# Compressor's first matrix: which operand is stationary, and in how many column tiles of the array

## The chip, the cores and the metric

The kernel runs on one core of one Trainium2 chip. The metric is the device time of one execution in microseconds (us), and lower is better. TensorE appears in the profile twice, as PE (its matmuls) and PEld (its weight loads). VectorE is DVE, ScalarE is ACT, and SyncE is SP, which here issues nearly all of the loads from HBM.

## The reference, cut to what matters

The program computes two blocks of two layers each, on 256 tokens of width 1024. Only the first block holds the part that is changed, and it holds it once per layer. In both of its layers a "compressor" turns overlapping blocks of 32 tokens into one key and one value per block:

```
def compress(kv, pe, w1, w2):
    B, G, T, dh = kv.shape                       # G = 2, T = 256, dh = 64
    NC = (T - CMP_BLOCK) // CMP_STRIDE + 1       # 15 blocks, length 32, stride 16
    idx = jnp.arange(NC)[:, None] * CMP_STRIDE + jnp.arange(CMP_BLOCK)[None, :]
    blocks = kv[:, :, idx, :] + pe
    flat = blocks.reshape(B, G, NC, CMP_BLOCK * dh)
    return jax.nn.silu(flat @ w1) @ w2           # w1: 2048 x 128, w2: 128 x 64
```

It is called once for the keys and once for the values, each with its own matrices. The two results feed the compressed attention. Beside it each layer has a gated recurrence (HGRN2, in 16 "level" steps below), selected and window attention, three gates (`hgo`, `hz`, `nz`) that are projections of the same input, and an output projection.

## The kernel before, in words

**Tiles and panels.** Activations lie transposed, with features on the 128 partitions and the 256 tokens along the free dimension. Weights come from HBM in panels of 1 MB through three raw slots (`SLOTS`). SP loads them in one fixed order (`LOADS`, load loop with `load_panel`, L2049). A panel can be loaded only when the one three places before it has left its slot (`slot_empty`, L2040). SP issues in order, so a load that waits for its slot holds up all later ones. Most panels are split after landing: ACT casts the high part (`high_part`, L1062) and DVE subtracts the low part (`low_part`, L1531). The split panels are used in three matmuls per product (L419 to L421). The two panels of the compressor's first matrix, `cmp0` (keys) and `cmp1` (values), are used unsplit, as plain float32. They give their raw slots back when the compressor's matmuls have ended (`release`, L381). In the load order `cmp0` and `cmp1` are followed by `hgo0`, `hgo1`, `hz0`, `hz1`, so the load of `hgo1` waits for `cmp0`'s slot, and `hz0` waits for `cmp1`'s.

**Who sets the order.** PE's program is written out by hand. Where PE has finished a piece that another engine must pick up, it appends an entry to an agenda with `todo` (L576). ACT and DVE each walk the agenda in the same order (L1201 and L1669). After an entry each of them also splits the panels whose slots are free at that place (`split_high`, L1073, and `split_low`, L1539). A split whose panel has not landed blocks the engine, and with it all later entries of the agenda.

**The stage around the change.** PE's order in a layer is: projections of queries and keys, with level steps (`level`, L601) strewn between them by `some` (L637); sums of squares; then the compressor's first matrix (`hid`, L699 to L711); one level step (the 14th); the query rotation `qr` (L716 and L717, waiting for DVE's products); one level step (the 15th); the key rotation `kr` (L724 and L725); a half panel of `hgo0` (`gate_chunk`, L619); the last level step; the other half of `hgo0`; the matmuls across the two chunks (`cross`, L734); and the compressor's second matrix (L742 and after, waiting for `hidden_ready`, L740). A level step on PE needs the step two before it to be finished by DVE (`level`, L1637). The first half of `hgo0` is written to PSUM bank 1, so it waits for ACT's copy of `qr0` out of that bank.

**The compressor's first matrix.** The token blocks lie in `M2`, part of the tile that the trace calls probs_t: for each of keys and values, 16 pieces of 128 rows by 32 columns (two groups by 16 block places). For each piece the 128x128 weight piece is stationary and the 32 columns move. Sixteen such matmuls add up in 32 columns of PSUM bank 3, with the hidden features on the partitions. After it the agenda entry `hidden` makes ACT take an exponential of the 64 columns (L1233) and DVE form the SiLU and a copy of it for the values (L1712 to L1722).

A float32 matmul appears in the trace as two weight loads and two matmuls, so 32 matmuls give 64 records in each layer.

Of the kernel before, what the change touches and what calls it, by code (L numbers as in the profile page):

```python
# [8 lines left out]
P = 128  # L9
# [33 lines left out]
def const_table():  # L43

    p = np.arange(P)
    parts = [("ident", np.eye(P)), ("ones", np.ones((P, P))),
             ("head_ones", (p[:, None] // 64 == p[None, :] // 64).astype(float))]

    rot = np.zeros((P, P))
    for h in (0, 64):  # L50
        for d in range(8):
            rot[h + 8 + d, h + d] = -1.0
            rot[h + d, h + 8 + d] = 1.0
    parts.append(("rot", rot))
    inv = (np.float32(500000.0) ** (-np.arange(0, 16, 2, dtype=np.float32) / np.float32(16))).astype(np.float32)
    ang = np.arange(T, dtype=np.float32)[None, :] * inv[:, None]
    cos, sin = np.ones((P, T)), np.zeros((P, T))
    for h in (0, 8, 64, 72):
        cos[h:h + 8] = np.cos(ang.astype(np.float32))
        sin[h:h + 8] = np.sin(ang.astype(np.float32))  # L60
    parts += [("cos", cos), ("sin", sin)]
    t = p[:, None, None] + P * np.arange(NT)[None, :, None]
    seen = (16 * np.arange(16)[None, None, :] + 31 <= t).astype(float)
    parts += [("cmp_neg", ((1 - seen) * NEG).reshape(P, NT * 16)), ("cmp_seen", seen.reshape(P, NT * 16))]
    parts.append(("head16", (p[:, None] // 16 == np.arange(8)[None, :]).astype(float)))
    parts.append(("upper", (p[:, None] <= p[None, :]).astype(float)))
    parts.append(("causal_neg", np.where(p[None, :] > p[:, None], NEG, 0.0)))
    at = 0
    for name, a in parts:
        CONST_COLS[name] = (at, a.shape[1])  # L70
        at += a.shape[1]
    levels = [(p[:, None] == p[None, :])]
    for n in range(1, NLVL):
        h = 1 << (n - 1)
        levels.append((p[:, None] // (2 * h) == p[None, :] // (2 * h)) & (p[:, None] % (2 * h) < h)
                      & (p[None, :] % (2 * h) >= h))
    masks = np.stack(levels, axis=1).astype(np.int32).reshape(P, NLVL * P)
    return np.concatenate([a for _, a in parts], axis=1).astype(np.float32), masks
# [69 lines left out]
def build(nc, a, out):  # L148
# [4 lines left out]
    with ExitStack() as ctx:  # L153
        def sb(name, cols, dt=F32):
            return ctx.enter_context(nc.sbuf_tensor(name, [P, cols], dt))
# [66 lines left out]
        NM = sb("neg_max", 8)  # L222
        SM = sb("prob_sums", 8)
        PP = FK
        ZR = sb("zeros", P)
        NT16 = sb("head_stats", 16)

# [57 lines left out]
        def bank(name):  # L285
            return ps[fills[name][0]]
# [74 lines left out]
        def _(pe):  # L361
# [219 lines left out]
            for l in range(DEPTH):  # L581
# [115 lines left out]
                some(1)  # L697

                pe.wait_ge(blocks_ready, l + 1)  # L699
                begin(f"hid_{l}", 3)  # L700
                for kv in range(2):
                    landed((f"cmp{kv}", l))
                    w1 = raw_panel((f"cmp{kv}", l), 16, P)
                    for jj in range(16):
                        ins = pe.matmul(ps[3][:, kv * 32:(kv + 1) * 32], w1[:, jj, :], M2[:, kv, jj, :, :],  # L705
                                        start=(jj == 0), stop=(jj == 15))
                done(f"hid_{l}", ins)
                release(("cmp0", l))
                release(("cmp1", l))
                todo(("hidden",))  # L710
                some(1)  # L711

                pe.wait_ge(rope_ready, l + 1)
                for j in range(2):
# [4 lines left out]
                                                 start=False, stop=True))  # L719
                    todo(("copy", f"qr{j}"))  # L720
                some(1)
                pe.wait_ge(k_rope_ready, l + 1)
                begin(f"kr_{l}", 4)
                pe.matmul(ps[4][:, :], ident, UK[:, 0:512], start=True, stop=False)  # L724
# [320 lines left out]
        def _(act):  # L1045
# [128 lines left out]
            for l in range(DEPTH):  # L1174
# [26 lines left out]
                for place, step, *arg in agenda[l]:  # L1201
# [6 lines left out]
                    elif step == "blocks":  # L1208

                        name = f"kcvc_{l}"  # L1210
                        full(act, name)
                        src = v3(bank(name), 2)
                        for g in range(2):
                            s = src[64 * g:64 * g + 64]
                            nc.scalar.copy(K2[0:64, :, g, :], s)
                            ins = nc.scalar.copy(K2[64:128, :, g, 0:T - 1], s[:, :, 1:T])
                        ins.then_inc(free(name), 1)
                    elif step == "k_square":
                        name = f"ks_{l}"
                        copy_out(name, KN[:, :], bank(name)[:, :])  # L1220
                        drained(act, name)
                        f(UK[:, 0:512], KN[:, :], ACT.Square).then_inc(ksq_ready, 1)
                    elif step == "gates":
                        name = f"vw_{l}"
                        full(act, name)
                        src = bank(name)[:, 0:304].rearrange("p (n w) -> p n w", n=NT)
                        nc.scalar.copy(vt[:, 1, :, :], src[:, :, 0:P])
                        f(gates, src[:, :, P:152], ACT.Exp, scale=-1.0).then_inc(free(name), 1)
                    elif step == "q_norm":
                        head_rinv([f"qss{j}_{l}" for j in range(2)], HZ[:, :], 64, 1024).then_inc(q_rinv_ready, 1)  # L1230
                    elif step == "k_norm":
                        head_rinv([f"kss_{l}"], UK[:, 512:1024], 64, 512).then_inc(k_rinv_ready, 1)
                    elif step == "hidden":  # L1233
                        full(act, f"hid_{l}")
                        f(SS[:, 0:64], bank(f"hid_{l}")[:, 0:64], ACT.Exp, scale=-1.0).then_inc(hid_exp_ready, 1)
                    elif step == "k_pad":

                        name = f"kr_{l}"
                        full(act, name)
                        src = v3(bank(name), 2)  # L1240
                        for g in range(2):
                            s = src[64 * g:64 * g + 64]
                            nc.scalar.copy(kz[0:64, :, 0, g, :], s)
                            ins = nc.scalar.copy(kz[64:128, :, 1, g, :], s)
                        ins.then_inc(free(name), 1)
                    elif step == "cross":
                        copy_out(f"cross_{l}", AC[:, :], bank(f"cross_{l}")[:, :])
                    elif step == "cmp_kv":
                        name = f"kc_{l}"
                        copy_out(name, KC[:, 0:32], bank(name)[:, 0:32])  # L1250
                        drained(act, name)
                        f(KC[:, 32:64], KC[:, 0:32], ACT.Square).then_inc(kcsq_ready, 1)
                    elif step == "o_square":
                        for g in range(2):
                            copy_out(f"o{g}_{l}", QP[:, g * 512:(g + 1) * 512], bank(f"o{g}_{l}")[:, :])
                        drained(act, f"o1_{l}")
                        f(SQ[:, 0:1024], QP[:, :], ACT.Square).then_inc(osq_ready, 1)
                    elif step == "kc_norm":
                        head_rinv([f"kcss_{l}"], SS[:, 64:96], 64, 32).then_inc(kc_rinv_ready, 1)
                    elif step == "o_norm":  # L1260
                        act.wait_ge(rope_ready, l + 1)
                        head_rinv([f"oss{g}_{l}" for g in range(2)], UK[:, :], P, 1024).then_inc(o_rinv_ready, 1)
                    elif step == "cmp_softmax":
                        act.wait_ge(cmp_shift_ready, l + 1)
                        f(SC[:, :], SC[:, :], ACT.Exp).then_inc(cmp_exp_ready, 1)
                    elif step == "scores":
                        exps(f"n{l}", arg[0], 8 * l + arg[0])
                    elif step == "turned":
                        turned_copies(f"n{l}", arg[0], 8 * l + arg[0])
                    elif step == "sigmoids":  # L1270
                        drained(act, f"hz1_{l}")
                        for dst, src in ((FG, HZ), (SG, SG)):
                            f(dst[:, :], src[:, :], ACT.Sigmoid).then_inc(sig_ready, 1)
                    elif step == "on":
                        mixed_high(l, None, (0, 1))
                        drained(act, f"nz1_{l}")
                        f(VH[:, :], NZ[:, :], ACT.Sigmoid).then_inc(sig_ready, 1)
                        mixed_high(l, [f"on{g}_{l}" for g in range(2)], (2, 3))
# [878 lines left out]
```

## Time and profile before

| what | value |
|---|---|
| runs | 1193.64, 1197.81, 1198.2 us; median 1197.81 us |
| the profiled execution | span 1197.1 us from its first to its last instruction; its time is not given apart from the span |
| busy share of the span | PE 93%, PEld 87%, DVE 59%, ACT 48% |
| mean granted TensorE clock | 0.953 of full speed |
| DMA | 163.88 MB, 137 GB/s on average |
| instructions | 19879 |

A busy share is an average over stages with different limits, and a matmul's modelled end lies after the start of the next one. So the time of a string of matmuls is read here from start to start. The granted clock is 1.00 at 2.4 GHz and 0.50 at 1.2 GHz.

### The profile page before, as it was taken

What the parts mean: (1) busy time and instruction counts of PE and PEld (TensorE: products, weight loads), DVE (VectorE), ACT (ScalarE), POOL (GpSimd) and SP (SyncE); (2) the same over time, 40 slices, a digit from 0 to 9 for tenths busy, and PEclk for the clock granted to TensorE, in tenths of its full rate; (3) what the DMA queues carried; (4) which work ended last, traced back from release to release, by engine and by line L of the source; (5) the groups of instructions that cost most, each with busy time, mean ns of one, the idle gap of its engine ahead of it and who ended that gap; (6) DMA issues with size and microseconds to landing.
All of it is one profiled execution on the core that took longest, in us unless ns stands there. A gap on an engine that the chain in (4) does not pass through costs nothing.

```text
span 1197.1 us, 19879 instructions
## 1 busy us (share of the span) xinstructions
PE 1108.9 (93%) x8321; PEld 1037.9 (87%) x8321; DVE 704.2 (59%) x1009; ACT 579.7 (48%) x816; POOL 4.9 (0%) x13
## 2 busy tenths in 40 slices
PE   4999898798999889798989999999799999999997
PEld 4999676698999677798988999999786699999996
DVE  5556445647566445548685766666543646766674
ACT  4542435546432445545753644544542636455453
POOL 1000000000000000000000000000000000000000
PEclk8999899899998899899999999999996999999998
DMA  8541613135531612134554555556243323655530
GB/s 278 176 113 36 211 36 106 36 106 177 183 107 36 211 62 80 53 121 150 179 176 141 177 176 184 193 184 194 76 146 119 127 91 122 211 176 183 193 115 36
DMA packets 144740, 163.88 MB, mean 137 GB/s; under 512 B 6072, under 2 KB 135424, under 8 KB 144672
## 3 DMA queue, kind: packets, MB, share of 16 engines
q1 hardware_dynamic: 143752, 161.46, 42.0%
q8 instruction: 52, 0.85, 0.3%
q10 hardware_dynamic: 632, 1.29, 0.3%
q0 software_dynamic: 288, 0.14, 0.0%
q14 instruction: 16, 0.13, 0.0%
HBM read 161.84 MB, written 1.05 MB: 136 GB/s over the span
## 4 chain that ended last, share of the span: by engine, by line
PE 74%; DVE 11%; ACT 9%; DMA 2%; issue 2%; SPq 1%; ACTq 0%; DVEq 0%
PE ps L419 21%; PE ps L421 21%; PE ps L420 21%; DVE panels_low L1534 3%; ACT panels_high L1069 3%; PE ps L612 2%; PE ps L499 2%; ACT probs L1055 2%; PE ps L705 2%; PE ps L435 1%; DMA panels<-in_w_in 1%; DVE neg_max L1555 1%; DVE probs L1570 1%; PE ps L523 1%; PE ps L505 1%
## 5 line engine op out<-in xcount | busy, mean ns | idle before, releaser
L419 PE MATMUL ps<-input_high,panels_low 128*128 128x256 f32 x1792 | 523.6, 292 | 33.4 <-DVE input_low L1514 14.2
L420 PE MATMUL ps<-input_low,panels_high 128*128 128x256 f32 x1792 | 515.4, 288 | 0.0
L421 PE MATMUL ps<-input_high,panels_high 128*128 128x256 f32 x1792 | 515.4, 288 | 0.0
L1534 DVE TENSOR_TENSOR panels_low<-panels,panels_high 128x2048 fp32r<-128x2048 f32 (+1 forms) x146 | 330.3, 2265 | 287.5 <-ACT panels_high L1069 279.8
L419 PEld LDWEIGHTS ps<-input_high,panels_low 128*128 128x128 f32 x1792 | 352.1, 196 | 44.5 <-issue 31.2
L420 PEld LDWEIGHTS ps<-input_low,panels_high 128*128 128x128 f32 x1792 | 352.3, 197 | 0.8 <-issue 0.5
L421 PEld LDWEIGHTS ps<-input_high,panels_high 128*128 128x128 f32 x1792 | 351.9, 196 | 0.0
L1069 ACT CAST panels_high<-panels 128x2048 fp32r<-128x2048 f32 (+1 forms) x146 | 274.7, 1883 | 152.3 <-PE ps L421 133.2
L419 PE MATMUL ps<-ffn_hidden_high,panels_low 128*128 128x256 f32 x352 | 100.3, 285 | 4.0 <-DVE ffn_hidden_low L2014 4.0
L420 PE MATMUL ps<-ffn_hidden_low,panels_high 128*128 128x256 f32 x352 | 99.7, 283 | 0.0
L421 PE MATMUL ps<-ffn_hidden_high,panels_high 128*128 128x256 f32 x352 | 99.7, 283 | 0.0
L419 PEld LDWEIGHTS ps<-ffn_hidden_high,panels_low 128*128 128x128 f32 x352 | 67.3, 191 | 4.4 <-issue 4.3
L420 PEld LDWEIGHTS ps<-ffn_hidden_low,panels_high 128*128 128x128 f32 x352 | 67.3, 191 | 0.1
L421 PEld LDWEIGHTS ps<-ffn_hidden_high,panels_high 128*128 128x128 f32 x352 | 67.2, 191 | 0.0
L1055 ACT ACTIVATE probs<-ps,neg_max 128x128 f32<-128x128 f32 (+1 forms) x80 | 32.5, 419 | 71.2 <-DVE neg_max L1555 71.2
L1055 ACT ACTIVATE squares<-residual 128x512 f32<-128x512 f32 x36 | 22.2, 629 | 79.5 <-DVE residual L1580 74.9
L419 PE MATMUL ps<-panels_high,input_low 128*128 128x256 f32 (+2 forms) x192 | 55.5, 289 | 0.0
L420 PE MATMUL ps<-panels_low,input_high 128*128 128x256 f32 (+2 forms) x192 | 55.1, 287 | 0.0
L421 PE MATMUL ps<-panels_high,input_high 128*128 128x256 f32 (+2 forms) x192 | 54.9, 286 | 0.0
L1518 DVE SCALAR_TENSOR_TENSOR squares<-residual,vectors,rinv 128x256 f32<-128x256 f32 x72 | 33.4, 481 | 25.8 <-ACT rinv L1055 25.8
L2000 DVE SCALAR_TENSOR_TENSOR gate_o<-ps,vectors,gate_o 128x255 f32<-128x255 f32 (+1 forms) x96 | 39.6, 475 | 9.6 <-ACT gate_o L1055 8.3
L523 PE MATMUL ps<-k_padded,q_rope 128*128 128x256 f32 (+1 forms) x80 | 35.3, 536 | 9.3 <-ACT probs L1055 7.0
(267 smaller groups left out, 1174.7 us busy)
## 6 DMA issues: line engine op xcount, KB each, us to landing
panels<-in_ffn_up SPq DMA_DIRECT2D x44, 1024.0 KB, 5.1
panels<-in_w_in SPq DMA_DIRECT2D x32, 1024.0 KB, 5.7
panels<-in_ffn_down SPq DMA_DIRECT2D x22, 1024.0 KB, 4.8
panels<-in_mix_w_in SPq DMA_DIRECT2D x20, 1024.0 KB, 5.3
panels<-in_w_out SPq DMA_DIRECT2D x8, 1024.0 KB, 5.3
panels<-in_w_pg SPq DMA_DIRECT2D x8, 1024.0 KB, 6.1
panels<-in_mix_w_out SPq DMA_DIRECT2D x8, 1024.0 KB, 5.8
panels<-in_w_pp SPq DMA_DIRECT2D x2, 1024.0 KB, 4.9
```

What stands on the lines that cost most here:

```text
L419: pe.matmul(dst, w[1], x[0], start=start, stop=False if not kw else True, **kw)
L420: pe.matmul(dst, w[0], x[1], start=False, stop=False if not kw else True, **kw)
L421: return pe.matmul(dst, w[0], x[0], start=False, stop=stop, **kw)
L499: ins = pe.matmul(ps[b][:, 0:T], ones, sq3[:, c, :], start=(c == 0), stop=(c == ND - 1))
L523: pe.matmul(o, q[:, n * P:(n + 1) * P], keys[:, :, 0:w], start=True, stop=True)
L612: ins = pe.matmul(ps[b][:, j * P:(j + 1) * P], KQ[:, s:s + P], QP[:, s:s + P], start=True, stop=True)
L705: ins = pe.matmul(ps[3][:, kv * 32:(kv + 1) * 32], w1[:, jj, :], M2[:, kv, jj, :, :], start=(jj == 0), stop=(jj == 15))
L1055: return nc.scalar.activation(dst, src, func, **kw)
L1069: nc.scalar.copy(high_slots[slot][:, 0:size], raw[n % SLOTS][:, 0:size]).then_inc(high_ready, 1)
L1518: V.scalar_tensor_tensor(xf3[:, c, :], h3[:, c, :], vec(gain, g0 + c), RINV[:, :], ALU.mult, ALU.mult).then_inc(xf_ready, 1)
L1534: V.tensor_tensor(low_slots[slot][:, 0:size], raw[n % SLOTS][:, 0:size], high_slots[slot][:, 0:size].bitcast(F32), ALU.subtract).then_inc( ...
L2000: ins = V.scalar_tensor_tensor(d, ps[2 * par + half][:, j * T:(j + 1) * T - back], VC[:, bass.ds(m + (w0 + (2 - back) * 2 * NFF), 1)], d, ...
```

## The change

The token blocks become the stationary operand and the weights move. A stationary piece has 32 columns and fills one of four column tiles of the array, at columns 0, 32, 64 and 96 (`tile_position`). Piece `jj` goes to tile `jj % 4`, so that each tile adds up four of the sixteen pieces, for keys and then for values. The results are four parts, on four groups of 32 partitions and in 128 columns per kind. ACT copies the 128x256 result to SBUF (agenda entry `hidden_parts`, into 256 columns of a tile that is written only later in the layer). After the query rotation and the 15th level step, two more matmuls per layer, with the copy as stationary operand and a 0/1 matrix of 32 columns moving, add the four parts and turn the result, so that it has the same form as before. The panels are released after the first set of matmuls. The entry `hidden` moves behind the two new matmuls. The table of constants grows by 32 columns.

```
+    parts.append(("sum_of_four", (p[:, None] % 32 == np.arange(32)[None, :]).astype(float)))
...
+        HP = NZ[:, 0:256]
...
-                begin(f"hid_{l}", 3)
+                begin(f"hid4_{l}", 3)
                 for kv in range(2):
                     landed((f"cmp{kv}", l))
                     w1 = raw_panel((f"cmp{kv}", l), 16, P)
                     for jj in range(16):
-                        ins = pe.matmul(ps[3][:, kv * 32:(kv + 1) * 32], w1[:, jj, :], M2[:, kv, jj, :, :],
-                                        start=(jj == 0), stop=(jj == 15))
-                done(f"hid_{l}", ins)
+                        c = 32 * (jj % 4)
+                        ins = pe.matmul(ps[3][c:c + 32, kv * P:(kv + 1) * P], M2[:, kv, jj, :, :], w1[:, jj, :],
+                                        start=(jj < 4), stop=(jj >= 12), tile_position=(0, c), skip_group_check=True)
+                done(f"hid4_{l}", ins)
                 release(("cmp0", l))
                 release(("cmp1", l))
-                todo(("hidden",))
+                todo(("hidden_parts",))
                 some(1)
...
+                drained(pe, f"hid4_{l}")
+                begin(f"hid_{l}", 3)
+                for kv in range(2):
+                    ins = pe.matmul(ps[3][:, kv * 32:(kv + 1) * 32], HP[:, kv * P:(kv + 1) * P],
+                                    const("sum_of_four"), start=True, stop=True)
+                done(f"hid_{l}", ins)
+                todo(("hidden",))
                 pe.wait_ge(k_rope_ready, l + 1)
...
+                    elif step == "hidden_parts":
+                        copy_out(f"hid4_{l}", HP, bank(f"hid4_{l}")[:, 0:256])
```

## Rows read from the trace of the kernel before

**Rows 1.** The page: the chain that ended last, by line.

```profile
PE ps L419 21%; PE ps L421 21%; PE ps L420 21%; DVE panels_low L1534 3%; ACT panels_high L1069 3%; PE ps L612 2%; PE ps L499 2%; ACT probs L1055 2%; PE ps L705 2%; PE ps L435 1%; DMA panels<-in_w_in 1%; DVE neg_max L1555 1%; DVE probs L1570 1%; PE ps L523 1%; PE ps L505 1%
```

**Rows 2.** The chain of waits in both layers' stages: start us, us, what.

```profile
109.96 0.86 PE ps L505 x2
110.82 0.89 PE ps L612 x8
...
121.41 0.38 SPq L2062
121.83 7.75 DMA panels<-in_w_in
129.61 1.91 ACT panels_high L1069
...
378.08 9.80 PE ps L705 x64
```

**Rows 3.** PE's timeline in the first layer: start us, us, instructions, idle before.

```profile
111.55 9.83 PE L705 MATMUL ps<-probs_t,panels 128*128 128x32 f32 x64
121.19 2.06 PE L612 MATMUL ps<-query,forget_key 128*128 128x128 f32 x8
...
129.72 1.02 PE L725 MATMUL ps<-k_rope_terms,consts 128*128 128x512 f32 x2
132.04 0.39 PE L419 MATMUL ps<-input_high,panels_low 128*128 128x256 f32 x1 [1.30 <-ACT q_rope L1060]
...
139.12 1.05 PE L734 MATMUL ps<-query,forget_key 128*128 128x128 f32 x8
...
142.29 0.46 PE L754 MATMUL ps<-decay_diag,values_hg 128*128 128x128 f32 x2 [1.72 <-issue]
```

**Rows 4.** Windows: busy time of PE, PEld, DVE, ACT, POOL; granted clock, DMA, GB/s.

```profile
111.50:115.80 4.30, 4.30 (x41) 4.30 (x41) 4.26 (x7) 0.68 (x2) 0.00 (x0) 1.00 0.00 0
115.80:121.20 5.40, 5.40 (x28) 5.40 (x27) 3.60 (x9) 0.00 (x0) 0.00 (x0) 0.50 0.00 0
121.20:126.00 4.80, 4.80 (x13) 3.19 (x14) 1.20 (x4) 0.22 (x1) 0.00 (x0) 0.50 0.76 236
126.00:131.00 5.00, 4.74 (x17) 2.23 (x15) 2.29 (x1) 3.29 (x2) 0.00 (x0) 1.00 1.10 348
...
140.00:150.00 10.00, 6.49 (x42) 6.27 (x41) 3.38 (x4) 5.13 (x9) 0.00 (x0) 0.83 0.31 105
```

**Rows 5.** ACT's and DVE's timelines in the first layer's stage.

```profile
131.41 1.07 ACT L1060 COPY q_rope<-ps 128x512 f32<-128x512 f32 x2
...
115.54 0.42 DVE L1663 TENSOR_TENSOR forget_key<-forget_key,gate_o 128x256 f32<-128x256 f32 x1
...
121.67 0.20 DVE L1715 TENSOR_SCALAR small<-small 128x64 f32<-128x64 f32 x1 [2.24 <-ACT small L1055]
...
122.75 0.23 DVE L1720 COPY cmp_hidden_rep<-cmp_hidden 128x128 f32<-128x128 f32 x1
...
137.41 0.42 DVE L1663 TENSOR_TENSOR forget_key<-forget_key,gate_o 128x256 f32<-128x256 f32 x1
```

**Rows 6.** Two 64-column tiles: PEld's timeline, one window, and PE's timeline.

```profile
949.93 1.73 PEld L907 LDWEIGHTS ps<-decay_diag,q_nope 128*64 128x64 f32 x32 [0.17 <-issue]
...
949.90:951.60 1.70, 1.70 (x31) 1.67 (x32) 0.76 (x1) 1.68 (x4) 0.00 (x0) 1.00 0.00 0
...
951.73 0.65 PE L551 MATMUL ps<-probs_t,values_hg 128*64 128x256 f32 x4
952.17 0.43 PE L553 MATMUL ps<-probs_t,values_hg 128*64 128x128 f32 x4
```

**Rows 7.** Single operations: a narrow moving operand, a copy out of PSUM, the constants' load.

```profile
L774 PE MATMUL ps<-cmp_k_padded,q_nope 128*128 128x32 f32 x32 | 3.7, 271 | 0.0
...
107.35 0.37 ACT L1227 COPY values_nsa<-ps 128x256 f32<-128x256 f32 x1 [4.96 <-PE ps L421]
...
consts<-in_const_table ACTq DMA_DIRECT2D x1, 676.0 KB, 6.0
```

## The prediction

> **What bounds the kernel now.** I read the page first. The span is 1197.1 us, as the table above has it, and the chain that ended last is mostly PE's three-matmul products; the compressor's line L705 has 2% of it [rows 1]. A line on the chain can be worth its whole time only if nothing else is waiting behind it, so I went on to the chain in order of time around L705, once per layer.
>
> There the reader sees a stage of its own. PE runs the 64 records of L705 from 111.55 to about 121.4 us in the first layer, and for 9.8 us in the second [rows 2, 3]. At 121.41 SP at last issues the loads that waited for the slots of `cmp0` and `cmp1`; 7.75 us of DMA and a cast of 1.91 us follow on the chain [rows 2]. DMA is idle while L705 runs, 0.00 busy, and saturated right after it [rows 4]. ACT sits behind those landings in its agenda, copies `qr0` at 131.41 [rows 5], and only then does PE get bank 1 and start `hgo0` at 132.04, after an idle 1.30 us [rows 3]. So the end of L705 starts a fixed sequence: 121.4 (its end) to 132.04 is 10.6 us, nearly all of it transfers and casts. What ends L705 earlier moves all of it.
>
> The windows give the price of L705 itself: 4.3 us at the full clock with 41 records started, then 5.4 us at half the clock [rows 4]. Its records are about 0.11 us apart at full clock although only 32 columns move: another narrow one, L774, takes 3.7/32 = 0.116 us [rows 7]. A 128x128 weight load per record sets that pace. The clock fell to 1.2 GHz in the middle of it, and came back only at 126.0 during the query rotation [rows 4].
>
> **The change part by part.**
>
> *The matmuls.* There are still 64 records per layer, now with 32 stationary and 128 moving columns. No record before has four tiles at once, so I bound it by neighbours. Alone, a 128-column record takes 0.111 us at full clock (0.89 for 8 [rows 2]): 64 x 0.111 = 7.1 us. Two 64-column tiles are in the trace: 31 records of L907, of the same 128 moving columns, start within 1.70 us, 0.055 apart, so each tile takes one per 0.11 us and the two run together [rows 6]. With four tiles that would be 64/4 x 0.111 = 1.8 us; with two at a time 3.5 us. I take four, because L907 shows a tile to keep its own pace whatever its neighbour does. L551 and L553 say the same: in program order they alternate by tile (two records of L551, two of L553, then the same for the other tile), but all four records of L551 start ahead of all four of L553 [rows 6]. So the tiles don't queue behind each other in program order. I add 0.2 us for entering the tiled arrangement: L907's first weight load has 0.17 us idle before it [rows 6]. So `hid4` takes 2.0 us and ends at 111.55 + 2.0 = 113.6. The Trainium skill, "TensorEngine Tiling (Array Packing)", section "Key Properties", says that a change of tiling mode drains TensorE; that 0.17 us agrees in kind, and is its whole price here.
>
> *The loads.* They are issued at 113.6 in place of 121.4. If nothing else is late, `hgo0` starts 10.6 us later, at 124.2, which is 7.8 us earlier than before.
>
> *What is late next.* PE itself, by a little. The 14th level step needs DVE's 12th, which ends at 115.54 + 0.42 = 115.96 [rows 5]. So PE idles about 2.4 us after `hid4`. From there its work up to `hgo0` is at full clock 2 x 0.89 (level steps) + 6 x 0.86 (rotations; the row has two 512-column records) = 6.9 us [rows 2]; before, the same ran from 121.19 to 130.74, 9.55 us, half of it at 1.2 GHz [rows 3, 4]. The two new matmuls add 4 records x 0.116 = 0.5 us [rows 7]. At full clock PE is through at 115.96 + 7.4 = 123.4, ahead of the 124.2. With as much slow clock as before it is through at 115.96 + 9.55 + 0.5 = 126.0. Which? The 10 us around the idle 1.72 us at 140.6 had a mean of 0.83, that is 3.4 us at 1.2 GHz [rows 3, 4]. 2.4 us of idle should do the same: 3.4 us at half clock cost 1.7 us of dense work. So PE is through at 125.1 and `hgo0` starts 132.04 - 125.1 = 6.9 us earlier (ends: 6.0 and 7.8).
>
> *The copy* of 128x256 costs about 0.37 us [rows 7]. It lies beside the 2.4 us in which PE waits for DVE, and ACT has nothing then: its agenda puts it ahead of the casts that block on the landings. The new wait of PE for it, after the 15th level step, finds it long done. If it were behind the casts, PE would stop there until 123 or later.
>
> *The moved `hidden`.* ACT's exponential now comes after the two copies of `qr`, and ahead of the copies for the padded keys, which are needed much later. DVE's four operations ran in slack, from 121.67 to 122.98, 1.3 us [rows 5]. They move behind the blocking low parts and between its last two level steps. DVE's last level step ended at 137.83 [rows 5], PE's `hgo0` at 139.12 [rows 3]: the slack of 1.29 us covers it just so. I cost it at 0, at most 0.2 us. The second matrix waits for `hidden_ready` only after `cross`, so it meets no new wait.
>
> *The table of constants* grows from 676 KB, 6.0 us to landing, by 16 KB, or 2.4% [rows 7]. That is at most 0.15 us, in the shadow of other first loads; 0.
>
> *Second layer.* The stage repeats, with 9.80 us of L705 on the chain [rows 2]; I take the same gain.
>
> **Sum.** 2 x 6.9 = 13.8, with the small costs 13.8 to 14: I say 13.8. From the profiled execution's own span, 1197.1, that gives 1183.3. What lies around the span is untouched and not shown apart. The runs' median is 0.7 us above that span, so I forecast 1184.0 us.
>
> **The rivals.**
>
> *Two at a time.* The Trainium skill, "TensorE: Matmul & The Clock Gate", section "The mechanism" under Part 3, says that matmuls start and end in program order. By that rule the second record of a tile would hold back the first of the next one. As a mechanism here: only neighbouring records of different tiles overlap, 64 x 0.055 = 3.5 us with the entry 3.7, `hid4` ends at 115.3, and the clock has no idle stretch to fall in. `hgo0` starts at 115.3 + 10.6 = 125.9, 6.1 us earlier: 12.2 in all, 1185.6 us. L551 ahead of L553 [rows 6] speaks against the order, but only for two tiles. 24%.
>
> *One at a time* (the tiling does not do what it says with four tiles): 7.1 us at full clock, `hid4` ends at 118.9, `hgo0` at 129.5, 2.5 us earlier, 5 in all: 1192.8 us. L907 speaks against it. 12%.
>
> *Slower.* The tiles don't overlap, and the narrow stationary operands count as little work, so that the clock is low in the whole stretch: 64 records x 0.222 = 14.2 us, which is 4.4 us per layer longer than 9.8, 8.8 in all: 1206.6 us. It decides from 9.83/64 = 0.154 us per record on. For it: the clock did fall in L705, with 128-column weights but little moving [rows 4]. Against it: in L907's 1.70 us the clock was 1.00 [rows 6], and the first 4.3 us here start at full clock. 4%.
>
> **How the numbers follow.** Four at a time has 58%: 1184.0 us, between 1182 (no slow clock) and 1186 (as much as before). Two at a time 24%, one at a time 12%, slower 4%; 2% remain for a wait that I don't see and that takes the gain. The range takes the first two cases and the spread of the runs (1193.6 to 1198.2, so up to 4 us below the median): 1180 to 1190; one at a time and slower lie outside. 0.5% is 6.0 us, about what a measurement of this kernel can tell from no change. The first two cases and a piece of the third are faster by more: 84%. Most of the third and the unseen wait are within it: 12%. Slower: 4%.
>
> **What would show it.** In the changed kernel: L705's successor with 64 records in about 2 us, four starting close together; SP's issue of the gate panels right after it; PE idle some 2.4 us ahead of the 14th level step; an ACT copy of 0.4 us next to that; `hgo0` starting 10.6 to 11.6 us after the end of `hid4`; DVE's `hidden` operations after its 15th level step. The span from the start of the compressor to `cross`, 27.6 us before [rows 3], should be near 20.7. I am wrong if the 64 records take over 4 us, if the new wait for ACT's copy holds PE, or if `hgo0` starts much later than 11.6 us after `hid4`.

## The result and the profile after

The changed kernel takes 1177.34 us (median of four runs, 1176.19 to 1178.79) against 1196.09 us for the kernel before in the same comparison (1193.64 to 1198.2). The ratio is 0.9849, with a 95% interval of 0.9829 to 0.9870. That is faster, as forecast, but 6.7 us below the forecast of 1184.0 us and outside the range of 1180 to 1190. The profiled execution of the changed kernel has a span of 1174.8 us and a time of 1176.69 us.

First the matmuls. PE's timeline of the changed kernel, in the first layer and in the second (start us, us, instructions, idle before), with the lines that answer to [rows 3]:

```profile
111.46 1.95 PE L708 MATMUL ps<-panels,probs_t 128*32 128x128 f32 x64
115.83 1.16 PE L614 MATMUL ps<-query,forget_key 128*128 128x128 f32 x8 [2.42 <-DVE forget_key L1675]
...
122.46 1.02 PE L735 MATMUL ps<-k_rope_terms,consts 128*128 128x512 f32 x2
124.22 0.39 PE L421 MATMUL ps<-input_high,panels_low 128*128 128x256 f32 x1 [0.73 <-ACT q_rope L1070]
...
131.29 1.06 PE L744 MATMUL ps<-query,forget_key 128*128 128x128 f32 x8
...
134.46 0.46 PE L764 MATMUL ps<-decay_diag,values_hg 128*128 128x128 f32 x2 [1.71 <-issue]
...
369.49 1.74 PE L708 MATMUL ps<-panels,probs_t 128*32 128x128 f32 x56
373.86 1.96 PE L614 MATMUL ps<-query,forget_key 128*128 128x128 f32 x8 [2.42 <-DVE forget_key L1675]
...
382.15 1.02 PE L735 MATMUL ps<-k_rope_terms,consts 128*128 128x512 f32 x2
382.61 0.68 PE L421 MATMUL ps<-input_high,panels_low 128*128 128x256 f32 x1
...
389.65 1.06 PE L744 MATMUL ps<-query,forget_key 128*128 128x128 f32 x8
```

(The view of the second layer ends at 371 us, so its L708 shows the first 56 of the 64 records.) The 64 records take 1.95 us in place of 9.83. PE then idles 2.42 us for DVE's level step, in both layers. `hgo0` starts at 124.22 instead of 132.04, and `cross` at 131.29 instead of 139.12.

The chain of waits behind L708 (start us, us, what) answers to [rows 2]:

```profile
111.53 1.93 PE ps L708 x64
...
113.48 0.38 SPq L2074
...
113.90 7.86 DMA panels<-in_w_in
...
121.78 1.91 ACT panels_high L1079
```

The sequence is the same as before with nearly the same durations (7.86 us of transfers against 7.75), and it begins 7.9 us earlier. From the end of L708 (111.46 + 1.95 = 113.41) to `hgo0` it takes 10.8 us; before it took 10.6.

ACT's and DVE's timelines (answering to [rows 5]) show the new copy in PE's idle time, and the moved `hidden` operations ahead of DVE's last level step:

```profile
113.48 0.37 ACT L1070 COPY nsa_z<-ps 128x256 f32<-128x256 f32 x1 [1.45 <-PE ps L708]
...
115.36 0.42 DVE L1675 TENSOR_TENSOR forget_key<-forget_key,gate_o 128x256 f32<-128x256 f32 x1
...
128.57 0.18 DVE L1727 TENSOR_SCALAR small<-small 128x64 f32<-128x64 f32 x1
...
129.63 0.23 DVE L1732 COPY cmp_hidden_rep<-cmp_hidden 128x128 f32<-128x128 f32 x1
...
130.72 0.42 DVE L1675 TENSOR_TENSOR forget_key<-forget_key,gate_o 128x256 f32<-128x256 f32 x1
```

The windows (columns as in [rows 4]) show the granted clock: the idle and the work up to `hgo0` in the first layer, then the idle, the work right behind it and the rest in the second.

```profile
111.40:113.40 2.00, 2.00 (x66) 1.69 (x64) 1.97 (x3) 0.63 (x1) 0.00 (x0) 1.00 0.00 0
113.40:115.80 2.40, 0.02 (x3) 0.00 (x0) 2.40 (x6) 0.37 (x1) 0.00 (x0) 1.00 0.43 101
115.80:124.20 8.40, 7.65 (x32) 4.43 (x32) 6.21 (x10) 4.32 (x4) 0.00 (x0) 1.00 1.08 348
...
371.40:373.80 2.40, 0.04 (x4) 0.00 (x0) 2.40 (x6) 0.37 (x1) 0.00 (x0) 1.00 0.42 92
373.80:377.40 3.60, 3.54 (x11) 2.51 (x12) 3.45 (x9) 0.53 (x1) 0.00 (x0) 0.53 1.09 369
377.40:383.00 5.60, 5.60 (x24) 3.22 (x22) 3.48 (x2) 4.37 (x5) 0.00 (x0) 1.00 1.04 304
```

In the first layer the clock stayed at 2.4 GHz after the idle. In the second it fell to 1.2 GHz for 3.4 of the 3.6 us after the same idle (a mean of 0.53). There `hgo0` starts 13.1 us after the first record of L708, in the first layer 12.8. This fall is not the rule: three more traces of the same kernel (e2, e11, e15) have the same idle of 2.41 to 2.42 us in both layers, and the clock stays at 1.00 behind it. Here is the window behind it in e2's second layer:

```profile
372.60:378.00 5.40, 5.39 (x26) 3.48 (x26) 3.99 (x9) 1.90 (x1) 0.00 (x0) 1.00 1.09 361
```

One measure is used for all experiments, the **stage**: the time from the first record of the compressor's first matrix to the first of `cross`, in layer 1 and layer 2, read from PE's timeline of each kernel.

| kernel | 64 records, layer 1 | stage, layer 1 | stage, layer 2 |
|---|---|---|---|
| before | 9.83 | 27.57 | 27.82 |
| before, again (e1, e12, e14) | 9.63 to 10.82 | 27.50 to 28.54 | 27.40 to 27.90 |
| after | 1.95 | 19.82 | 20.16 |
| after, again (e2, e11, e15) | 1.95 to 1.96 | 19.72 to 19.90 | 19.75 to 19.90 |
| e3 one tile | 7.17 | 27.33 | 26.22 |
| e4 two tiles | 3.69 | 22.58 | 22.77 |
| e6 tile by tile | 4.33 | 22.12 | 23.20 |
| e5 late loads | 1.96 | 30.21 | 31.81 |
| e7 late split | 1.95 | 18.50 | 20.16 |
| e8 filled idle | 1.95 | 16.01 | 16.01 |
| e9 spread split | 1.95 | 16.40 | 16.40 |

The two stages gave 7.75 + 7.66 = 15.4 us; the forecast was 13.8. But the two traced spans lie 22.3 us apart (1197.1 and 1174.8). The other 6.9 us lie where nothing was changed; e12 to e15 deal with them.

### The profile page after: what moved, and what is told of

Same layout as the page of the kernel before. It is cut to its first block, busy times and chain, and to the rows that moved or that the text cites. A ratio compares the mean times of both kernels' runs of the same rounds, so it can differ in the third digit from the quotient of the medians.

```text
span 1174.8 us, 19899 instructions
## 1 busy us (share of the span) xinstructions
PE 1083.4 (92%) x8329; PEld 1016.0 (86%) x8329; DVE 704.1 (60%) x1009; ACT 580.8 (49%) x818; POOL 5.0 (0%) x13
## 4 chain that ended last, share of the span: by engine, by line
PE 75%; DVE 12%; ACT 9%; issue 2%; DMA 1%; SPq 1%; DVEq 0%; ACTq 0%
PE ps L421 22%; PE ps L422 21%; PE ps L423 21%; DVE panels_low L1546 3%; ACT panels_high L1079 3%; PE ps L614 2%; PE ps L501 2%; ACT probs L1065 2%; PE ps L437 1%; DVE neg_max L1567 1%; DVE probs L1582 1%; PE ps L507 1%; PE ps L525 1%; DMA panels<-in_w_in 1%; PE ps L972 1%
```

## The experiments

**How many tiles run at once: e3, e4.** The rivals differed in this alone. Both experiments keep the operands of the change and use fewer tiles; the copy and the adding matmul shrink to the rows that are used.

```
-                        c = 32 * (jj % 4)
+                        c = 32 * (jj % 1)        # e4: jj % 2
...
-                                        start=(jj < 4), stop=(jj >= 12), tile_position=(0, c), skip_group_check=True)
+                                        start=(jj < 1), stop=(jj >= 15), tile_position=(0, c), skip_group_check=True)
```

> All sixteen pieces go to one 32-column tile, one after another. Theory (concurrency of tiles makes the gain, a tile takes a record per 0.111 us): the 64 records take 7.1 us, 5.2 us more than with four tiles, and the loads start that much later: 2 x 5.2 = 10.4 us slower than the change, near 1188. Rival (narrow stationary operands let the clock fall): the records take up to 14 us, over 20 us slower than the change. Rival (narrow operands alone make the gain, not the tiles side by side): within 2 us of the change.

> The pieces alternate between two 32-column tiles. Theory: 64 records at 0.055 us, 3.6 us, 1.7 us more than with four tiles; the loads decide, so 2 x 1.7 = 3.4 us slower than the change, near 1181. Rival (PE's wait for VectorE after the compressor hides it): within 1 us of the change, since PE idles 2.4 us there.

Measured: e3 1189.13 us, ratio 0.9961 (0.9944 to 0.9977); e4 1180.44 us, ratio 0.9882 (0.9855 to 0.9908). Against the changed kernel beside them (e2, 1176.79 us) that is 12.3 us more where 10.4 was expected, and 3.7 us more where 3.4 was. PE's timeline and two windows of e3:

```profile
111.78 7.17 PE L708 MATMUL ps<-panels,probs_t 128*32 128x128 f32 x64
...
129.71 0.58 PE L421 MATMUL ps<-input_high,panels_low 128*128 128x256 f32 x1 [2.86 <-ACT q_rope L1070]
```

```profile
111.80:119.00 7.20, 7.20 (x66) 7.00 (x66) 7.13 (x14) 0.56 (x2) 0.00 (x0) 1.00 0.00 0
129.70:136.00 6.30, 6.29 (x30) 6.29 (x31) 5.55 (x12) 2.77 (x6) 0.00 (x0) 0.52 1.03 323
```

PE's timeline of e4:

```profile
112.28 3.69 PE L708 MATMUL ps<-panels,probs_t 128*32 128x128 f32 x64
...
126.63 0.39 PE L421 MATMUL ps<-input_high,panels_low 128*128 128x256 f32 x1 [2.02 <-ACT q_rope L1070]
```

One tile, two tiles and four take 7.17, 3.69 and 1.95 us: each tile takes a record per 0.11 us, and four tiles are 7.17/1.95 = 3.7 times as fast as one. The slower rival's premise falls as well: with a stationary operand of 32 columns the clock is 1.00 for all of e3's 7.2 us. Before, with 128 stationary and 32 moving columns, it fell after 4.3 us [rows 4].

e3's stage is the lesson that a shorter matmul is not yet a shorter stage. Its 64 records are 2.7 us shorter in layer 1, and `hgo0` indeed starts 2.6 us earlier after them (129.71 - 111.78 = 17.9 against 20.5). But PE has now waited 2.86 us for ACT's copy, and the clock behind it is 0.52, so that the stage as a whole is only 0.2 us shorter. In layer 2 it is 1.6 us shorter.

**Whether the order of issue matters: e6.** The same four tiles and the same 64 records, but four pieces in a row for one tile.

```
-                        c = 32 * (jj % 4)
+                        c = 32 * (jj // 4)
...
-                                        start=(jj < 4), stop=(jj >= 12), tile_position=(0, c), skip_group_check=True)
+                                        start=(jj % 4 == 0), stop=(jj % 4 == 3), tile_position=(0, c), skip_group_check=True)
```

> As the change, but piece jj goes to tile jj // 4, so that four matmuls in a row (eight records) sit on one tile before the next tile's come. Theory (tiles don't queue in program order, and PE looks far ahead): still about 2 us for the 64 records, time as the change. Rival (matmuls start in program order): tiles overlap only where one ends and the next begins, 64 records in 6 us or more, about 8 us slower than the change, near 1185.

Measured: 1183.07 us, ratio 0.9917 (0.9891 to 0.9943). PE's timeline of e6, the whole group and then only what starts up to 112.37:

```profile
111.92 4.33 PE L708 MATMUL ps<-panels,probs_t 128*32 128x128 f32 x64
...
111.92 0.62 PE L708 MATMUL ps<-panels,probs_t 128*32 128x128 f32 x4
```

PE's timeline of the changed kernel, only what starts up to 111.56:

```profile
111.46 0.32 PE L708 MATMUL ps<-panels,probs_t 128*32 128x128 f32 x4
```

In the changed kernel four records have started within 0.1 us. In e6 it takes 0.45 us for four, at the pace of a single tile. Eight records of one tile take 1.06 us from start to end (the eight of L744 above), so the eight runs of eight records follow each other at (4.33 - 1.06)/7 = 0.47 us, where a run alone holds its tile for 8 x 0.11 = 0.9 us. So neither expectation of 2 us nor of 6 us is met: the tiles do overlap, but a tile is reached only when the one ahead is about half through. A record of the second tile thus starts ahead of the first tile's last three, but not ahead of all of them. The interleaved order of the change is worth 4.33 - 1.95 = 2.4 us per layer.

**Where the gain comes from: e5.** The four tiles stay, but the slots of `cmp0` and `cmp1` are given back only after the two adding matmuls. ACT and DVE keep the place of their splits.

```
-                release(("cmp0", l))
-                release(("cmp1", l))
                 todo(("hidden_parts",))
...
                 done(f"hid_{l}", ins)
+                b, k = fills[f"hid_{l}"]
+                for kv in range(2):
+                    freed((f"cmp{kv}", l), (psum_full[b], k + 1), order_of[f"hid4_{l}"])
                 todo(("hidden",))
```

> As the change, but the two raw slots are given back only when the two matmuls that add the four parts have ended, some 8 us later; the casts keep their place in the agenda. PE's saving in the matmuls stays. Theory (the gain comes through the earlier loads): the gate panel's first half starts 8 us later, the whole gain of 15 us is gone, and PE's longer idle stretch ahead of it can drop the clock, up to 3 us more per layer: 1193 to 1199. Rival (PE's own saved time is the gain): within 3 us of the change, 1180 or less.

Measured: 1198.24 us, ratio 1.005 (1.003 to 1.007). SP's and PE's timelines of e5:

```profile
121.43 12.86 SPq L2075 DMA_DIRECT2D panels<-in_w_in  x5
...
132.11 0.58 PE L421 MATMUL ps<-input_high,panels_low 128*128 128x256 f32 x1 [8.91 <-ACT q_rope L1071]
```

With matmuls as fast as the change's, the whole gain is gone, and e5 is 6.3 us above the kernel before beside it (1191.93). SP issues at 121.43, where it did before (121.41 [rows 2]), `hgo0` starts at 132.11 (before 132.04), and PE idles 8.91 us there, with the clock at 0.50 behind it. What the change buys is the earlier release of two slots; the shorter matmuls are only the means.

**Whether the splits are the next limit: e7, e10.** In the changed kernel ACT's `qr` copies wait behind two casts that block on landings. Here the splits of `hgo1` and `hz0` come after the copies for the padded keys; the loads stay early. e10 is e7 once more, beside the changed kernel (e11).

```
-                release(("cmp0", l))
-                release(("cmp1", l))
+                b, k = fills[f"hid4_{l}"]
+                for kv in range(2):
+                    freed((f"cmp{kv}", l), (psum_full[b], k + 1), order_of[f"hid4_{l}"] + 6)
```

> As the change, but the two gate panels that follow the compressor are cast and subtracted after the padded keys, so that neither ScalarE's copies of the rotated queries nor VectorE's last level steps stand behind their landings. Theory (in the changed kernel the in-order casts behind the loads bind, and PE is only 0.5 us ahead of them): the gate panel starts when PE is through, near 123.4, and the last level steps no longer wait; 1.2 us per layer, 2.4 us faster than the change, near 1174.5. Rival (the loads themselves bind what follows): same time as the change.

> The version with the later splits once more, beside the change on one chip. Theory: 2 to 3 us faster than the change there. Rival (the first difference came from the chips or the clock's phase): no difference.

> The change once more, as the reference of the two runs above: 1175 to 1178 us, ratio to the kernel before between 0.985 and 0.987.

Measured: e7 1173.79 us, ratio 0.9848 (0.9811 to 0.9886); e10 1173.58 us, ratio 0.9845 (0.9817 to 0.9873), beside the changed kernel's 1175.83 us, ratio 0.9854 (0.9829 to 0.9879). PE's timeline of e7:

```profile
122.59 1.02 PE L736 MATMUL ps<-k_rope_terms,consts 128*128 128x512 f32 x2
123.05 0.68 PE L421 MATMUL ps<-input_high,panels_low 128*128 128x256 f32 x1
...
130.10 1.06 PE L745 MATMUL ps<-query,forget_key 128*128 128x128 f32 x8
```

The idle 0.73 us ahead of `hgo0` is gone, and layer 1's stage is 1.3 us shorter. Layer 2's is 20.16, in e10 too: there the clock fell to 0.51 for 3.4 us behind the idle, as in the changed kernel's first trace, and PE itself was late. In the changed kernel's other traces, where the clock stayed at 1.00, PE waited 0.64 to 0.81 us for ACT's copy in both layers. Beside each other, e10 is 2.25 us below the changed kernel, as expected, but the two intervals overlap, and the stages of e10 and e11 differ by only 39.54 - 38.66 = 0.9 us. So how much the later splits gain is not shown. Behind the shorter matmuls two things end nearly together: PE's own work and ACT's blocked copies.

**Whether PE's idle can be filled: e8, e9.** e8 is e7 with the first half of `hgo0` moved to the place right behind L708, into bank 6, where PE waited for DVE; ACT copies `hgo0` out only when the levels are ready. e9 is e8 with the three splits spread over the agenda.

```
                 todo(("hidden_parts",))
+                gate_chunk()
                 some(1)
...
                 todo(("k_pad",))
-                gate_chunk()
                 some(16)
...
-                    b = 1 if key[0] == "hgo0" else 0
+                    b = 6 if key[0] == "hgo0" else 0
...
-                for kv in range(2):                   # e9, against e8
-                    freed((f"cmp{kv}", l), (psum_full[b], k + 1), order_of[f"hid4_{l}"] + 6)
+                for kv, later in ((0, 5), (1, 11)):
+                    freed((f"cmp{kv}", l), (psum_full[b], k + 1), order_of[f"hid4_{l}"] + later)
...
-                        release(key)
+                        if key[0] == "hgo0":
+                            fb, fk = fills[f"hgo0_{l}"]
+                            freed(key, (psum_full[fb], fk + 1), order_of[f"hgo0_{l}"] + 6)
+                        else:
+                            release(key)
```

> As the run before, and the first half of the gate panel hgo0 moves into PE's idle 2.4 us right behind the compressor's matmuls, in PSUM bank 6. Theory: PE's 2.4 us are used and the second half starts as soon as the last level step is issued: cross-chunk matmuls 3.7 us earlier per layer, 7 us faster than the change, near 1169.5. Rival (VectorE's level steps or the clock bind instead): 1173 to 1176.

> As the filled version, but the three gate panels behind the compressor are split at three places: hgo1 after the hidden entry, hz0 after the second matrix's copies, hz1 after the compressed keys' norm, so that ScalarE's copy of the cross-chunk matmuls is not behind casts. Theory (in the filled version the gain of 3.9 us at the cross-chunk matmuls was given back in a 4.06 us wait for ScalarE's copy, which stood behind three casts): that wait falls to about 1.5 us, 2 to 3 us per layer less than the filled version: 1168 to 1171. Rival (the casts only move the wait to ScalarE's later copies or to VectorE): 1172 to 1175.

Measured: e8 1174.71 us, ratio 0.9866 (0.9824 to 0.9908); e9 1168.88 us, ratio 0.9794 (0.9768 to 0.9819). PE's and ACT's timelines of e8, and a window behind the wait:

```profile
127.33 1.06 PE L745 MATMUL ps<-query,forget_key 128*128 128x128 f32 x8
132.84 0.76 PE L765 MATMUL ps<-decay_diag,values_hg 128*128 128x128 f32 x2 [4.06 <-issue]
...
126.15 3.70 ACT L1080 CAST panels_high<-panels 128x2048 fp32r<-128x2048 f32 x2
...
130.36 1.90 ACT L1080 CAST panels_high<-panels 128x2048 fp32r<-128x2048 f32 x1
132.16 0.59 ACT L1071 COPY decay_cross<-ps 128x512 f32<-128x512 f32 x1
```

```profile
132.80:137.00 4.20, 4.16 (x19) 4.19 (x20) 2.57 (x2) 0.85 (x3) 0.00 (x0) 0.50 1.09 366
```

PE's and ACT's timelines of e9:

```profile
112.57 1.95 PE L712 MATMUL ps<-panels,probs_t 128*32 128x128 f32 x64
...
128.97 1.16 PE L749 MATMUL ps<-query,forget_key 128*128 128x128 f32 x8 [0.23 <-DVE forget_key L1682]
...
130.85 0.46 PE L769 MATMUL ps<-decay_diag,values_hg 128*128 128x128 f32 x2 [0.33 <-issue]
...
130.17 0.59 ACT L1075 COPY decay_cross<-ps 128x512 f32<-128x512 f32 x1 [0.63 <-PE ps L749]
```

In e8 `cross` starts 3.8 us earlier in the stage than in the changed kernel (16.01 against 19.82), as expected, but the time is the rival's, and nearly all of the gain is lost right behind `cross`. ACT's copy of `cross` stands behind three casts and ends at 132.75, so PE idles 4.06 us where the changed kernel has 1.71: 2.35 us are gone. Behind the longer idle the clock is 0.50 until 138.9, for 6.1 us; the changed kernel has 3.4 us at 0.50 behind its own wait (a mean of 0.57 from 134.5 to 138.5). The difference of 2.7 us costs dense work some 1.3 us (an estimate). In e9 the casts lie elsewhere, the copy starts 0.63 us after ACT fell idle, and PE waits 0.33 us. e9 beats both kernels, by 6.9 us against the changed kernel beside it (1168.88 and 1175.83).

**The time outside the stages: e1, e2, e12 to e15.** The remaining 6.9 us between the two traces lie in unchanged work. e1, e12 and e14 are the kernel before, unchanged; e2 and e15 the changed one, unchanged. e13 is the kernel before with the new constants alone:

```
     parts.append(("head16", (p[:, None] // 16 == np.arange(8)[None, :]).astype(float)))
+    parts.append(("sum_of_four", (p[:, None] % 32 == np.arange(32)[None, :]).astype(float)))
     parts.append(("upper", (p[:, None] <= p[None, :]).astype(float)))
```

> The kernel before, unchanged, to see how its granted clock and its time vary between executions. Theory (the gain beyond the two compressor stages is granted clock elsewhere): the time moves with the mean clock over several us, some executions near 1194 and some near 1198, and the trace shows half-clock stretches in the second block in other places or of other length than the first trace did. Rival (the gain beyond the stages is a fixed effect of the change): executions agree within 1 us, with the same half-clock stretches.

> The changed kernel, unchanged. Theory: 1176 to 1179 us, the stage from the start of the compressor to the cross-chunk matmuls again near 20 us per layer against 27.7 before, the time beyond 2 x 7.7 = 15.4 us of gain moving with the clock. Rival: always 18 us below the kernel before, with the clock's half-speed stretches in the same places as in the first trace.

> The kernel before once more, for a trace of a faster execution. Theory (executions differ by granted clock, not by work): an execution near 1190 to 1193 shows a higher mean clock, near 0.961, with the same busy counts and shorter half-clock stretches in the second block, and the two compressor stages as long as before, 27.6 us each. Rival: the stages themselves are shorter in a fast execution, and the 15 us are an artefact of a slow one.

> The kernel before with the 32 new columns of constants and nothing else: they are loaded and never read, and every tile behind them in SBUF lies 128 bytes further on. In the kernels that have the change (whatever their stage) the stretch of the second block that lasts 87.2 to 89.3 us in three executions of before lasts 84.3 to 84.8, and the stretch from 600 to 740 us lasts 140.4 against 140.0. Theory A, that the shifted addresses do this: 84.3 to 84.8 and 140.4 here too, a time 2 to 5 us below before. Theory B, that it is the granted clock, which falls at an idle of PE in one execution and not in another for reasons outside the change's operations: 87 to 89.5 and 140.0, a ratio of 0.998 to 1.002. Either way the compressor's stages stay at 27 to 28.5 us.

> The kernel before, a fourth execution with a profile. Theory A (addresses): the second block's stretch is 87 to 89.5 us as in the three others. Theory B (the clock by chance): it can be anything from 84.3 to 89.5.

> The changed kernel, a fourth execution with a profile, 1175 to 1179 us. Theory A: the second block's stretch is 84.3 to 84.8 us again. Theory B: it can be anything up to 89.5.

Measured: e1 1192.38 us, ratio 0.9996 (0.9981 to 1.0011); e2 1176.79 us, ratio 0.9860 (0.9837 to 0.9884); e12 1190.36 us; e13 1193.53 us, ratio 1.001 (0.9993 to 1.0027); e14 1190.91 us; e15 1174.46 us. The medians of the kernel before that stood beside these runs were 1193.6 us (23 runs), 1191.93 (15), 1192.27 (11) and 1191.6 (13). The profiled executions (span, mean granted clock), first the trace of before that the forecast was made from:

```profile
core 0: 1197.1 us, clock 0.953
```

then e1 and e12:

```profile
core 0: 1196.8 us, clock 0.952
```

```profile
core 0: 1188.5 us, clock 0.961
```

The changed kernel's traces have 1174.8 us at 0.969, 1175.0 at 0.970 (e2), 1175.1 at 0.970 (e11) and 1172.6 at 0.971 (e15). One kernel, with not one instruction changed, has executions 8.6 us apart in span, and the shorter one has the higher mean clock. e14 is like e12 (1189.1 us, 0.961). The trace that the forecast was made from was one of the long ones. e1's span of 1196.8 goes with a time of 1198.78 us, e12's of 1188.5 with 1190.36: the time is about 1.9 us above the span.

The windows of one stretch of the second block, the same work each time, show a place where some 5 of the 6.9 us lie: first the trace of before,

```profile
877.00:966.70 89.70, 81.45 (x515) 63.06 (x515) 42.09 (x55) 38.63 (x70) 0.00 (x0) 0.85 0.37 118
```

then e14, e13, the changed kernel and e9:

```profile
873.00:960.20 87.20, 78.59 (x511) 62.44 (x510) 42.08 (x55) 38.27 (x69) 0.00 (x0) 0.88 0.38 121
```

```profile
874.50:959.20 84.70, 75.13 (x512) 59.37 (x511) 41.99 (x55) 38.26 (x69) 0.00 (x0) 0.94 0.39 125
```

```profile
860.60:944.90 84.30, 74.72 (x509) 58.93 (x509) 41.97 (x54) 38.27 (x69) 0.00 (x0) 0.94 0.39 125
```

```profile
848.60:935.70 87.10, 78.46 (x510) 62.30 (x509) 42.09 (x55) 38.30 (x69) 0.00 (x0) 0.88 0.38 121
```

In e13, with the table of constants alone, this stretch takes 84.7 us at a clock of 0.94, close to the changed kernel's 84.3 (e15: 84.5). That was the expectation of theory A. But e9, which has the same constants, takes 87.1 us at 0.88, like e14. So the constants alone do not decide it. In the twelve traces with the constants that are short here (84.3 to 84.8 us) the clock's first fall in the stretch begins 25.4 to 26.0 us into it; in e9, e12 and e14, which take 87 us, it begins 26.1 to 26.3 us into it, and a second fall of 10.2 us follows. And the whole execution of e13 is not shorter: its span is 1189.1 us, as e14's, and its ratio is 1.001, as theory B expected. Neither theory holds as a whole.

The table does have one small fixed effect. The other stretch that e13's expectation names, from about 600 to 740 us, runs at a clock of 1.00 in every trace. It takes 140.0 to 140.1 us in the four traces of before, and 140.4 us in e13 and in all twelve traces with the change. Why it does is not shown.

Against e14, a short execution of before, the changed kernel's span is 14.3 us shorter, and the stages differ by 28.54 + 27.42 - 19.82 - 20.16 = 16.0. Between e14 and e15, which ran on one chip, the spans differ by 16.5 us and the stages by 28.54 + 27.42 - 19.84 - 19.90 = 16.2. To within 2 us the stages account for the change's gain; the rest between the first two traces is how long the traced execution of before happened to be. Which executions get the lower clock, and why, stays open.

## Why the prediction was right in direction and too small

**The matmuls: right.** 2.0 us forecast, 1.95 measured, and the matmuls of the rivals of two tiles and one were priced right (3.7 and 7.1 forecast; 3.69 and 7.17 in e4 and e3). That the sum came out this close is in part luck. It was 1.8 us for the records and 0.2 for entering the tiled arrangement. The measured 1.95 is 1.68 us from the first start to the last and 0.27 us that the last record takes; the entry lies ahead of it, and L708 starts 0.20 us after the record before it, where those records are 0.11 apart, so it costs 0.09. The rule that matmuls start and end in program order, from the Trainium skill, "TensorE: Matmul & The Clock Gate", section "The mechanism", stood beside the rival of two tiles at a time. These traces disagree with it: a float32 matmul is two records on one tile, and one tile takes a record per 0.11 us (e3), yet four records start within 0.1 us, and in e6 the second tile starts ahead of three records that stand before it in the program. e6 shows that the order of issue still counts. The same page of the Trainium skill, section "Measured speedup vs the span model", has 2.38 times for three column tiles; four gave 3.7 times here.

**The loads: right.** Issue at 113.6 forecast, 113.48 measured; 10.6 us from there to `hgo0` forecast, 10.7 measured in layer 1. The rivals' sums put `hgo0` 14.35 us (two tiles) and 17.95 us (one tile) after the first record; e4 and e3 have 14.35 and 17.9. e5 confirms that this is the gain's way.

**What is late next: half right, and the first step that failed.** The idle of PE was forecast at 2.4 us and is 2.42. But the step went on: "2.4 us of idle should do the same: 3.4 us at half clock cost 1.7 us of dense work." In layer 1 the clock stayed at 1.00, and `hgo0` came 7.7 us earlier, the forecast's upper end nearly. In layer 2 the clock did fall, and the size of the cost was right: the second matmul of the key rotation (L735) starts 12.66 us after L708, against 11.00 in layer 1, so 1.66 us later. Yet `hgo0` came only 0.36 us later than in layer 1 (13.12 and 12.76), because PE's wait ahead of `hgo0` takes the other 1.30 (`hgo0` starts 0.46 us after L735 in layer 2, 1.76 in layer 1). The forecast put `hgo0` at 125.1 in place of the loads' 124.2, so 0.9 us per layer; it measured 0 and 0.4. What failed is that this idle was taken to make the clock fall each time: it did so in one of the eight places in the four traces of the changed kernel. What makes it fall in one place and not in another stays open. That is 15.4 in place of 13.8, or 1.6 of the 6.7 us.

**The copy, the moved operations, the constants: right.** The copy takes 0.37 us inside PE's idle. DVE's last level step ends at 131.14 and `cross` starts at 131.29: the cover did just so. The constants measured 1.001 (0.9993 to 1.0027) in e13.

**The sum's baseline: the step that failed most.** "The runs' median is 0.7 us above that span, so I forecast 1184.0 us." A time is about 1.9 us above its own span, so the traced execution took about 1199 us, more than any of the three runs shown, and two of those three were themselves high: later medians of 11 to 23 runs are 1191.6 to 1193.6. Which executions were caught was chance. With the measured 15.4 us, 1177.34 + 15.4 = 1192.7 is the baseline that fits, 5.1 us under the one used; the 1196.09 us beside the result lie 3.4 us above it as well. The 1193.64 among the three runs hinted at it, and the range allowed for it only in part: it took 4 us off the forecast at its lower end, with nothing for a stage better than forecast.

**The chances** went to the right case, four tiles at once.

## What to carry to other kernels

Look for what a slow small operation holds back: here 7.9 us of matmuls was worth 7.7 us because two buffers came free behind it, and without that release (e5) nothing. Column tiles paid off fully here when neighbouring instructions in the program went to different tiles. Before subtracting a gain from a traced execution, ask where that execution stands among the kernel's own, by its time and mean granted clock; filling an idle engine paid here only when the queue behind it (ACT's casts) was rearranged as well (e8 and e9).

## What the runs showed that was not expected

- Four tiles of 32 columns run side by side at nearly the full pace of each (7.17 us in one tile, 3.69 in two, 1.95 in four), but issued tile by tile the same records take 4.33 us.
- With a narrow stationary operand the clock stayed at 1.00 for 7.2 us (e3), where in the trace of before, with a narrow moving operand, it fell to 0.50 after 4.3 us [rows 4].
- The same idle of 2.42 us before the same work left the clock at 1.00 in one layer, and in the next it was 0.53 behind it; in three more traces it stayed at 1.00 in both.
- Thirty-two unread columns of constants lengthen one stretch of 140.0 us at full clock to 140.4, in each of the 13 traces that have them. The whole kernel measured the same with them (ratio 1.001).
